# Attention on one core: three rotating PSUM banks for transposed probabilities and reciprocals, with some steps moved in their queues

## The reference

```python
score = sum_h w[q, h] * relu(q_idx[q, h] . k_idx[l])     # indexer, causal
idx   = top_k(score, 256)                                # keys kept per query
logits = q . k_sel * HEAD_DIM ** -0.5 + rel_bias[rel_bucket(dist)]
probs = softmax(where(dist >= 0, logits, -inf))          # 8 heads, 4 kv heads
out   = probs @ v_sel                                    # (1024, 8 * 64)
```

## Time and profile before

| what | value |
| --- | --- |
| three runs, median (lowest to highest) | 1610.19 us (1607.29 to 1610.98) |
| the profiled execution: its time, its span | 1606.7 us, 1605.0 us |
| mean granted TensorE clock | 0.983 of full speed |
| TensorE, VectorE, ScalarE, GpSimd busy | 96%, 60%, 36%, 38% of the span |
| up to the attention | 487.7 us, TensorE busy 455.67 |
| attention, 487.70 to 629.50 us | 141.8 us, TensorE busy 124.85, VectorE 86.79, ScalarE 79.79, GpSimd 39.21 |
| merge, output, norm, 629.50 to 899.30 us | 269.8 us, TensorE busy 260.38 |
| feed-forward, 899.30 us to the end | 705.7 us, TensorE busy 694.04 |

### The profile page before, as it was taken

One profiled execution on the slowest core, in us unless ns is written; L12 is line 12 of the kernel. 1 busy time (PEld: TensorE's weight loads), 2 busy tenths in 40 slices (PEclk: granted clock), 3 DMA queues, 4 the chain that ended last, 5 costly groups with the idle time before them and its releaser, 6 DMA issues.

```text
span 1605.0 us, 25832 instructions
## 1 busy us (share of the span) xinstructions
PE 1534.9 (96%) x9489; PEld 1378.1 (86%) x9489; DVE 964.5 (60%) x2173; ACT 572.7 (36%) x1171; POOL 606.2 (38%) x548
## 2 busy tenths in 40 slices
PE   6998999989998898999999999999999999999997
PEld 5863566658995666999999999999999999999996
DVE  6327989898996665132537745555554455555545
ACT  4324354335315555212434522313224223132233
POOL 4111019284544221111122825537336255273350
PEclk9999999997998999999999999999999999999999
DMA  5431011141210012221012201102102011021002
GB/s 176 108 102 53 21 41 27 37 115 47 53 40 2 1 37 63 80 68 59 27 40 79 80 20 61 52 27 78 50 29 78 20 58 52 26 78 50 28 13 107
DMA packets 91556, 87.60 MB, mean 55 GB/s; under 512 B 17046, under 2 KB 82214, under 8 KB 91469
## 3 DMA queue, kind: packets, MB, share of 16 engines
q1 hardware_dynamic: 83671, 75.45, 15.4%
q0 software_dynamic: 2688, 8.39, 1.8%
q10 hardware_dynamic: 5118, 2.69, 0.6%
HBM read 78.30 MB, written 8.45 MB: 54 GB/s over the span
## 4 chain that ended last, share of the span: by engine, by line
PE 57%; DVE 1%; POOL 1%; issue 1%; ACT 0%; DMA 0%; DVEq 0%; POOLq 0%
PE banks L2010 27%; PE banks L2107 15%; PE banks L108 13%; PE banks L1967 0%; PE banks L1948 0%; PE banks L2124 0%; DVE yo L2584 0%; POOL wL L2158 0%; DMA out_dram<-yo 0%; ACT XH L2226 0%; POOL hnL_lo L2171 0%; DVE hnL_hi L2439 0%; POOL dL L2155 0%; POOL T4L L2171 0%; ACT sH L2219 0%
## 5 line engine op out<-in xcount | busy, mean ns | idle before, releaser
L2158 POOL TENSOR_TENSOR wL<-w_raw,wH 128x512 fp32r<-128x512 f32 x176 | 231.2, 1330 | 315.1 <-ACT wH L2269 314.0
L2010 PE MATMUL banks<-hnH,wH 128*128 128x344 f32 x704 | 225.9, 321 | 2.2 <-POOL wL L2158 0.8
L2010 PE MATMUL banks<-hnH,wL 128*128 128x344 f32 x704 | 224.7, 319 | 0.0
L2571 DVE TENSOR_TENSOR resid<-resid,banks 128x344 f32<-128x344 f32 x264 | 132.0, 511 | 96.8 <-PE banks L2107 96.8
L2107 PE MATMUL banks<-aH,dH 128*128 128x344 f32 x528 | 169.2, 320 | 0.0
L2107 PE MATMUL banks<-aH,dL 128*128 128x344 f32 x528 | 169.1, 320 | 0.0
L2107 PE MATMUL banks<-aL,dH 128*128 128x344 f32 x528 | 168.2, 319 | 0.0
L1463 DVE TENSOR_SCALAR_CACHE_REDUCE pta<-SC,thr 128x384 uint8<-128x384 f32 (+4 forms) x160 | 144.0, 930 | 2.2 <-POOL SC L905 0.2
L2269 ACT ACTIVATE wH<-w_raw 128x512 fp32r<-128x512 f32 x176 | 109.6, 626 | 73.3 <-PE banks L2010 40.5
L2010 PEld LDWEIGHTS banks<-hnH,wH 128*128 128x128 f32 x704 | 132.2, 188 | 3.2 <-issue 1.9
L2010 PEld LDWEIGHTS banks<-hnH,wL 128*128 128x128 f32 x704 | 132.2, 188 | 0.0
(11 more groups left out here) (408 smaller groups left out, 3638.3 us busy)
## 6 DMA issues: line engine op xcount, KB each, us to landing
w_raw<-in_w_gate_up_dram SPq DMA_DIRECT2D x22, 1024.0 KB, 5.0
d_raw<-in_w_down_dram SPq DMA_DIRECT2D x11, 1024.0 KB, 4.9
big<-in_w_in_dram SPq DMA_DIRECT2D x12, 512.0 KB, 4.0
W<-in_x_prompt_dram SPq DMA_DIRECT2D x8, 512.0 KB, 5.6
slab_raw<-in_w_in_dram SPq DMA_DIRECT2D x8, 512.0 KB, 4.2
x_nat<-in_x_prompt_dram SPq DMA_DIRECT2D x8, 512.0 KB, 4.2
slab_raw<-in_w_out_dram SPq DMA_DIRECT2D x8, 512.0 KB, 3.8
out_dram<-yo SPq DMA_DIRECT2D x8, 512.0 KB, 3.5
```

The lines of the kernel that those rows point to most:

```text
L2010: last = mm(out, W_[w][s][:, i * P:(i + 1) * P], x_of(x)(i), start=start and i == 0 and j == 0, stop=stop and i == HALF - 1 and j == 2)
L2158: gp.tensor_tensor(wL[s].rearrange("p (k n) -> p k n", k=HALF), quadrant(x, *HOME[name]), f32(wH[s]).rearrange("p (k n) -> p k n", k=HALF) ...
L2571: V.tensor_tensor(resid[:, m, chunk(DOWN_ORDER[o])], resid[:, m, chunk(DOWN_ORDER[o])], ps[:, 4 + n % 4, 0:CH], ALU.add).then_inc(y_done, 1)
```

## The change

Transposed units and turned reciprocals get one common sequence of slots, and slot s takes bank 4, 5 or 7 in turn. Before TensorE writes slot s it waits for the copy of slot s - 3, whoever makes it. Even units are still copied by ScalarE and odd ones by VectorE. At a block's first pair ScalarE copies the reciprocals ahead of that pair's units, and VectorE does `out_block` ahead of them. For the last pair, `invert_sums` and `transpose_sums` come ahead of the copies and of the last product.

```diff
+            SLOT_BANKS = (4, 5, 7)
+            slots, unit_slot, sums_slot = [], [], []
+            for n in range(PAIRS + 1):
+                if n and n % 4 == 0:
+                    sums_slot.append(len(slots))
+                    slots.append(("rT", n // 4))
+                for b in range(pt_base(n), pt_base(n + 1) if n < PAIRS else pt_base(n)):
+                    unit_slot.append(len(slots))
+                    slots.append(("pt_v", b // 2 + 1) if b % 2 else ("pt_a", b // 2 + 1))
+
+            def slot_bank(s):
+                return SLOT_BANKS[s % 3]
@@ TensorE
+                def slot_emptied(s):
+                    if s >= 3:
+                        name, count = slots[s - 3]
+                        pe.wait_ge({"pt_a": pt_evac_a, "pt_v": pt_evac_v, "rT": rT_evac}[name], count)
+
                 def transpose_probs(n):
...
-                            if b >= 2:
-                                pe.wait_ge((pt_evac_a, pt_evac_v)[b % 2], b // 2)
+                            slot_emptied(unit_slot[b])
                             for j in range(4 * q, min(4 * q + 4, i + 1)):
-                                last = tr(ps[:, 4 + b % 2, j % 4 * P:j % 4 * P + P], lg[:, n % 2, f, j * P:(j + 1) * P], ident[:, :])
+                                last = tr(ps[:, slot_bank(unit_slot[b]), j % 4 * P:j % 4 * P + P], lg[:, n % 2, f, j * P:(j + 1) * P], ident[:, :])
...
                 def transpose_sums(i):
                     pe.wait_ge(ri_ready, i + 1)
-                    if i:
-                        pe.wait_ge(rT_evac, i)
+                    slot_emptied(sums_slot[i])
...
+                transpose_sums(NBLK - 1)
                 times_values(PAIRS - 1)
-                transpose_sums(NBLK - 1)
@@ ScalarE
+                def sums_out(i):
+                    act.wait_ge(rT_ready, i + 1)
+                    if i:
+                        act.wait_ge(o_evac, i)
+                    A(rinvT, ps[:, slot_bank(sums_slot[i]), :], ACT.Copy).then_inc(rT_evac, 1)
...
+                    if n and n % 4 == 0:
+                        sums_out(n // 4 - 1)
                     for f in range(2):
                         for q in range(PTB[i]):
...
-                            A(probsT[n % 2][:, f, q * 512:q * 512 + w], ps[:, 4, 0:w], ACT.Copy).then_inc(pt_evac_a, 1)
-                    if n and n % 4 == 0:
-                        act.wait_ge(rT_ready, n // 4)
-                        if n > 4:
-                            act.wait_ge(o_evac, n // 4 - 1)
-                        A(rinvT, ps[:, 7, :], ACT.Copy).then_inc(rT_evac, 1)
-                act.wait_ge(rT_ready, NBLK)
-                act.wait_ge(o_evac, NBLK - 1)
-                A(rinvT, ps[:, 7, :], ACT.Copy).then_inc(rT_evac, 1)
+                            A(probsT[n % 2][:, f, q * 512:q * 512 + w], ps[:, slot_bank(unit_slot[b]), 0:w], ACT.Copy).then_inc(pt_evac_a, 1)
+                sums_out(NBLK - 1)
@@ VectorE
                     if n + 1 < PAIRS:
                         row_min(n + 1)
+                    else:
+                        invert_sums(NBLK - 1)
+                    if n and n % 4 == 0:
+                        out_block(i - 1)
                     for f in range(2):
                         for q in range(PTB[i]):
...
-                            V.tensor_copy(probsT[n % 2][:, f, q * 512:q * 512 + w], ps[:, 5, 0:w]).then_inc(pt_evac_v, 1)
-                    if n and n % 4 == 0:
-                        out_block(i - 1)
-                invert_sums(NBLK - 1)
+                            V.tensor_copy(probsT[n % 2][:, f, q * 512:q * 512 + w], ps[:, slot_bank(unit_slot[b]), 0:w]).then_inc(pt_evac_v, 1)
                 out_block(NBLK - 1)
```

More of the change, by code:

```diff
@@ L829, in transpose_sums @@
                     pe.wait_ge(ri_ready, i + 1)
-                    if i:
-                        pe.wait_ge(rT_evac, i)
+                    slot_emptied(sums_slot[i])
                     for t in range(4):
                         for f in range(2):
-                            last = mm(ps[f * HD:(f + 1) * HD, 7, t * P:(t + 1) * P], ri[:, 2 * t + f:2 * t + f + 1].to_broadcast([P, HD]),
+                            last = mm(ps[f * HD:(f + 1) * HD, slot_bank(sums_slot[i]), t * P:(t + 1) * P], ri[:, 2 * t + f:2 * t + f + 1].to_broadcast([P, HD]),
                                       ident[:, :], start=True, stop=True, tile_position=(0, f * HD))
```

## The result

The changed kernel takes 1594.3 us (median of 4 runs, 1593.0 to 1596.3) against 1610.6 for the kernel before (4 runs, 1607.3 to 1612.3): ratio 0.9905, 95% interval 0.9886 to 0.9923, or 12 to 18 us less. The forecast was 1597.6, range 1593.5 to 1603.0.

What follows compares the result with a forecast made beforehand. TensorE's queue with its holes was taken to bound the attention stage. Terms of 7.8, 3.2 and 1.6 us summed to 12.6, giving 1597.6 us against the median of 1610.2, range 1593.5 to 1603.0.

Steps and rivals of the forecast that it cites:

- The path: Attention stage: TensorE's queue with its holes sets it, and any gain before 629.50 us reaches the end one for one.
- Three banks: Blocks 4 to 7: unit 3 finds a third bank free, unit 4 waits instead; 7.8 us off, bounds 0 to 9.6.
- k = 4: Pairs with four transposes in the shorter unit: unit 4 does not wait, gain 1.43 - 1.02 = 0.41 us per pair.
- `out_block` and reciprocals ahead: Blocks' first pairs: TensorE's product no longer waits for the previous block's `out_block`; 3.2 us off, bounds 2.1 to 3.75.
- the first boundary: First block change: product still queues behind `out_block` and VectorE's copy, starting at 502.3, not 501.74; 0.55 us deducted.
- ScalarE's moved copy: Reciprocal copy ahead of the probability copy: its 0.60 us lie in ScalarE's idle time, so cost zero.
- The last sums: Stage end: sums ahead of the last product fill the wait for VectorE's copy; 1.6 us off, bounds 0.9 to 2.0.
- R1: Blocks 4 to 7: ScalarE's exponentials or VectorE's minima come late, bank gain lost partly or wholly, 1601.5 or 1605.4 us; chance 0.16.
- R2: The wait only moves from unit 3 to unit 4 and `out_block` pays back in late copies; 1610 us; chance 0.06.
- R3: TensorE's clock falls to its lower level and back inside the attention stage; slower, near 1619 us; chance 0.06.

Runs made afterwards that it cites:

- after_again: The changed kernel again with its work unaltered, timed against the kernel before: ratio 0.9913; attention interval 126.46 us.
- order_only: Against the changed kernel: two alternating banks and a separate reciprocal bank as before, only the queue moves kept; ratio 0.9974 to the kernel before.
- after_3: A further trace of the changed kernel, work unaltered; one execution, 1595.2 us, attention interval 125.58 us.
- out_block_first: Against the kernel before: only VectorE's `out_block` moved ahead of its copies, ScalarE's reciprocal copy left behind its probability copies; ratio 1.0119.
- last_only: Against the kernel before: only the end changed, last reciprocals inverted ahead of VectorE's last copies, last sums turned ahead of the last product; ratio 0.9997.
- banks_only: Against the changed kernel: three banks and early reciprocal copy kept, `out_block` behind VectorE's copies and the end as before; ratio 0.9940 to the kernel before.
- small_first: Against the changed kernel: in blocks 4 to 7 each head's shorter unit is turned first and copied by ScalarE; 1588.2 us, ratio 0.9877 to the kernel before.
- its extensions: small_first, and small_first with the product starting on the keys ScalarE copied; 1588.2 and 1590.3 us against the changed kernel's 1592.9.

## Why the prediction was right

*The path.* That the attention stage hangs on TensorE's queue and passes its gain on whole held: 12.8 us at the end of the stage, and 269.8 us from there to the feed-forward stage in before, 269.8 in after_again (616.56 to 886.32).

*Three banks, 7.8 us (0 to 9.6).* Measured 8.12, by the difference of changed kernel and order_only. The wait stood before unit 4 as said, and pairs of block 4 took 1.60 us for 1.57. Only k = 4 was mis-sized: 0.53 us per pair for 0.41, since sixteen unhindered transposes take 1.93 us and not 2.04. The 0.1275 us for each was read from a run of eight and carried the step to the next group in it: 1.02 us for eight and 1.93 for sixteen make 0.114 for each and 0.11 for the step.

*`out_block` and reciprocals ahead, 3.2 us (2.1 to 3.75).* In blocks 2 to 6 order_only measures 1.48 + 0.74 + 0.42 + 0.09 = 2.7, where 3.75 less the first boundary's 1.0 makes 2.75. At the first boundary 0.45 was forecast. The whole of that stretch moves by up to 1 us with the clock's rise, but the piece that holds the wait can be read: from the transposes of the block's first pair to those of its second 2.87 or 2.88 us pass in all four traces of before, and in the changed kernel 2.10 in three and 2.31 in after_3. So 0.56 to 0.77 us come off there, more where the clock rises late, and the forecast was a little low. That ScalarE's moved copy costs nothing held, as no wait for it is left on TensorE, and out_block_first shows what it is there for: without it the other move makes the interval 20 us longer.

*The last sums, 1.6 us (0.9 to 2.0).* 1.57 in last_only and in order_only, and 1.58 between banks_only and the changed kernel.

*The terms add.* banks_only's 9.8 us behind the first eight pairs are more than the bank term: it also recovers 1.7 of the `out_block` holes. The two causes share these holes, and in the changed kernel they count once, as the sum had it.

*The rivals.* R1 fell: in blocks 4 to 7 TensorE waits neither for exponentials nor for VectorE's copies, but for the 0.9 us at the pair before the last, which before had too, and small_first took 2.6 us more out before anything else came late. R2 fell by banks_only. R3 did not happen: the granted clock was 1.00 from 502 us to the end of the stage, through holes of about 0.3 us before unit 4 and one of 0.9. Behind holes of 2.2 to 2.6 us it did fall, in out_block_first. The Trainium skill (TensorE: Matmul & The Clock Gate, section A second HAM failure mode: psum-queue depth-cycling) tells of a kernel that cycled through PSUM banks and whose clock went back and forth between its levels. The rotation over three banks here does not bear that out.

*The median.* The forecast 1597.6 was 3.3 us above the result, although its sum was right to 0.2 us up to the end of the stage. The result lies only 0.8 us inside the range's lower end, so that it lies inside owes something to luck. Both comparisons (12 to 18 us, 12 to 16 us) hold the traces' 12.8. The four traces of each kernel differ in their mean spans by 13.5 us: 13.2 in the attention interval, 0.4 ahead of it and -0.1 behind it, and of the 13.2 some 0.8 are in the first eight pairs, where the clock rises. That the medians differ by 15 to 16 us I put down to clock spells, which differ between executions of one kernel; this is argued from traces that move by as much, not shown for the timed runs.

## What to carry to other kernels

Where a bank's cycle is transposes, copy, transposes, read the cycle from start to start and ask which unit takes the bank next: the gain of a further bank is the work that slips into the wait, capped by the wait. A step that another engine waits for goes ahead of the copies only together with everything that it waits for itself. And for changes of under 1%, cut the trace at repeated landmarks: segments agreed to 0.02 us between executions where times scattered by 5 us and more.

## What was not expected of the hardware

- The time until TensorE's clock rises at the start of the stage is not fixed. The first eight pairs took 18.66 to 19.55 us in six traces of the changed kernel and its extensions, which run the same work there.
- The clock fell behind quite short holes: in out_block_first TensorE waited 2.17 to 2.57 us at four places, each close behind a hole of 0.34 to 0.67 us, and behind the first of them the next logits took 2.51 us instead of 1.35. The fall about doubled the price of the wait (18.0 us lost in blocks 4 to 7, of them some 8.5 of waiting).
- Whether it falls at a given place can differ between executions of one kernel, for a reason that no run here shows. At 376 to 402 us it was at 0.61 to 0.67 in seven of fourteen traces and at 1.00 in seven; the 552 matmuls of the output stage took between 87.30 and 89.89 us.
